# Gate and up of a feed-forward as seven block products of half the columns, and the projection down in three parts

## The reference

```
y = swiglu(rmsnorm(h, pre_g), w_gu, w_down)     # (silu(u @ gate) * (u @ up)) @ w_down
h = h + 0.5 * rmsnorm(y, post_g)                # first block; in the second h = h + y
```

## Time and profile before

| | |
|---|---|
| median of 3 runs | 3500.77 us (3498.62 to 3511.09) |
| profiled execution | 3503.76 us |
| its span, first to last instruction | 3501.9 us |
| TensorE busy | 3446.2 us, 98% |
| VectorE busy | 1805.0 us, 52% |
| ScalarE busy | 1373.8 us, 39% |
| GpSimd busy | 340.5 us, 10% |

### The profile page before, as it was taken

One profiled execution on the slowest core, in us unless ns is written; L12 is line 12 of the kernel. 1 busy time (PEld: TensorE's weight loads), 2 busy tenths in 40 slices (PEclk: granted clock), 3 DMA queues, 4 the chain that ended last, 5 costly groups with the idle time before them and its releaser, 6 DMA issues.

```text
span 3501.9 us, 42768 instructions
## 1 busy us (share of the span) xinstructions
PE 3446.2 (98%) x17080; PEld 2869.9 (82%) x17080; DVE 1805.0 (52%) x3164; ACT 1373.8 (39%) x2437; POOL 340.5 (10%) x327
## 2 busy tenths in 40 slices
PE   8999999999999999999999999999999999999998
PEld 7888887878888888888887878888888888888887
DVE  5442665746544335442665656544348675644432
ACT  4222453635432234222453544432236373333221
POOL 0110110121011001110111021011000001201100
PEclk9999999999999999999999999999999999999999
DMA  4223342252232332223433253232323322323232
GB/s 139 96 93 96 99 113 79 70 139 88 88 102 96 91 96 91 95 93 95 117 82 91 65 150 94 79 103 96 95 79 93 88 77 69 106 90 102 96 89 74
DMA packets 110871, 332.23 MB, mean 95 GB/s; under 512 B 18248, under 2 KB 19016, under 8 KB 110672
## 3 DMA queue, kind: packets, MB, share of 16 engines
q1 hardware_dynamic: 98352, 306.82, 28.1%
q0 software_dynamic: 12320, 22.66, 3.1%
HBM read 306.23 MB, written 4.21 MB: 89 GB/s over the span
## 4 chain that ended last, share of the span: by engine, by line
PE 94%; DVE 2%; DMA 2%; ACT 2%; issue 1%; POOL 0%; SPq 0%; DVEq 0%; ACTq 0%
PE PS L706 92%; PE PS L1031 1%; DMA raw<-in_win 1%; ACT wh L1150 1%; DVE wl L1639 0%; DMA raw<-in_gu 0%; DVE stk L1920 0%; DMA tmp<-tmp 0%; ACT tmp L1150 0%; DVE tmp L1969 0%; DVE tmp L2347 0%; PE PS L1024 0%; ACT PT L1150 0%; ACT L1150 0%; DVE tmp L1987 0%
## 5 line engine op out<-in xcount | busy, mean ns | idle before, releaser
L706 PE MATMUL PS<-uh,wh 128*128 128x512 f32 (+1 forms) x3096 | 1180.7, 381 | 16.1 <-DVE ul L1667 11.9
L1639 DVE TENSOR_TENSOR wl<-raw,wh 128x1024 fp32r<-128x1024 f32 (+2 forms) x595 | 725.6, 1221 | 877.9 <-ACT wh L1150 875.7
L706 PE MATMUL PS<-uh,wl 128*128 128x512 f32 (+1 forms) x3096 | 1176.9, 380 | 0.0
L706 PE MATMUL PS<-ul,wh 128*128 128x512 f32 (+1 forms) x3096 | 1171.1, 378 | 0.0
L1150 ACT ACTIVATE wh<-raw 128x1024 fp32r<-128x1024 f32 (+2 forms) x595 | 584.1, 984 | 537.8 <-PE PS L706 494.0
L706 PEld LDWEIGHTS PS<-uh,wh 128*128 128x128 f32 x3096 | 583.9, 189 | 136.1 <-DVE wl L1639 10.2
L706 PEld LDWEIGHTS PS<-ul,wh 128*128 128x128 f32 x3096 | 584.6, 189 | 113.7
L706 PEld LDWEIGHTS PS<-uh,wl 128*128 128x128 f32 x3096 | 583.1, 188 | 110.4 <-issue 1.4
L706 PE MATMUL PS<-gh,wh 128*128 128x512 f32 (+1 forms) x968 | 363.6, 376 | 0.0
L706 PE MATMUL PS<-gh,wl 128*128 128x512 f32 (+1 forms) x968 | 362.1, 374 | 0.0
L706 PE MATMUL PS<-gl,wh 128*128 128x512 f32 (+1 forms) x968 | 359.6, 372 | 0.0
(11 more groups left out here) (223 smaller groups left out, 3664.4 us busy)
## 6 DMA issues: line engine op xcount, KB each, us to landing
raw<-in_gu SPq DMA_DIRECT2D x220, 512.0 KB, 3.4
raw<-in_win SPq DMA_DIRECT2D x139, 512.0 KB, 3.5
raw<-in_dn SPq DMA_DIRECT2D x80, 512.0 KB, 3.5
raw<-in_wbr SPq DMA_DIRECT2D x72, 256.0 KB, 2.6
raw<-in_dn SPq DMA_DIRECT2D x40, 384.0 KB, 3.1
raw<-in_wout SPq DMA_DIRECT2D x24, 512.0 KB, 3.4
raw<-in_wv SPq DMA_DIRECT2D x20, 512.0 KB, 3.5
stk<-stk SPq DMA_DIRECT2D x72, 128.0 KB, 2.6
```

Of the source, the lines that this page charges most:

```text
L706: return e.matmul(out, lhs, rhs, start=start, stop=stop, skip_group_check=True)
L1639: tt(wl[:, p % 4, 0:n], raw[:, p % 3, 0:n], wh[:, p % 4, 0:n], SUB).then_inc(*S.lo.up(("lo", p)))
```

## The change

For f = 0 to 3 (`PLAIN`) gate and up stay as they were. For f = 4 to 21 one `pair` replaces the two jobs. The weight is seen as 2x2 blocks: two halves of the depth (4 tiles each) by gate and up; the activation as 2x2 blocks: two halves of the depth by two halves of the tokens (256 each). Strassen's algorithm in Winograd's form gives the four result blocks from seven products in place of eight, each product 4 tiles deep and 256 columns wide: 12 matmuls of 256 columns. That takes sums of blocks on both sides.

* Activation side, once for each feed-forward: `scaled` (DVE) applies gain and `rb` beforehand, sixteen instructions of 256 columns; four sums of 1024 columns, two on DVE (`sum_of`) and two on POOL; seven splits of 1024 columns, high part on ACT (`high`), low part on DVE (`low_operand`).
* Weight side, for each pair: POOL makes four sums of 512 columns from the two loaded pieces (`sums`), and ACT and DVE split four "cuts" (first, sums12, sums43 of 1024 columns, last of 512) in place of two pieces.
* Result side, for each pair: ACT copies four partial results of 256 columns out of PSUM, DVE adds four times from PSUM with a copy, multiplies gate and up, and makes the low part as before. PE waits for some of the copies in the middle of a pair.

POOL's multiplication by `rb` stays for f = 0 to 3 alone. The `raw` ring has four buffers in place of three.

The projection down runs in three parts of depth 6, 8 and 8 (after f = 6, after f = 14, after f = 21; `PARTS`, `DEPTHS`), each part 8 jobs. Parts are added up in SBUF: ACT copies the first, DVE adds the second and third (`add_part`). The square for the norm reads SBUF, and the gain of the norm after the stage is no longer applied by ACT but by DVE in the passage between stages (a SCALAR_TENSOR_TENSOR in place of the TENSOR_TENSOR at L1701; in the passages after mixers too). `dn` 5, 6 and 7 are cut in halves, in place of `dn` 7 alone. Buffers are laid out anew to make room.

```diff
+            def pair(v, f):
+                job = JOBS["pair", v, f]
+                c, (a, b, g, d) = job.first, pair_banks(f)
+                def product(i, at, part, b, start):
+                    E.wait_ge(S.lo, "lo", c + at)
+                    E.wait_ge(S.dn, "operand", v, i)
+                    for k in range(4):
+                        s = 512 * part + P * k
+                        w1, w2 = wh[:, (c + at) % 4, s:s + P], wl[:, (c + at) % 4, s:s + P]
+                        x1, x2 = bh[:, i, 256 * k:256 * k + 256], bl[:, i, 256 * k:256 * k + 256]
+                        last = three(bank(b, 0, 256), w1, w2, x1, x2, start and k == 0, k == 3)
+                    return last
+                take(a, S.dv, "c22", v, f)
+                product(0, 0, 0, a, True).then_inc(*S.mm.up(("product", v, f, 1)))
...
+                product(2, 0, 1, g, True).then_inc(*S.mm.up(("product", v, f, 2), ("cut", c)))
+                E.wait_ge(S.aa, "copy", v, f, 0)
+                product(3, 1, 1, a, False).then_inc(*S.mm.up(("product", v, f, 6), ("cut", c + 1)))
...
 # ScalarE
+                for f in range(PLAIN, FT):
+                    c = JOBS["pair", v, f].first
+                    ahead(c + 2)
+                    copy(f, 0, 1)
+                    if f > PLAIN and f - 1 not in PARTS:
+                        high_g(f - 1)
+                    copy(f, 1, 5)
+                    ahead(c + 4)
+                    copy(f, 2, 6)
+                    ahead(c + 5)
+                    silu(f, ("c12", v, f))
+                    copy(f, 3, 4)
 # VectorE
+                    if i == 0:
+                        scaled(0)
+                        scaled(1)
+                    elif i == 2:
+                        sum_of(1)
+                        scaled(4)
+                        scaled(5)
+                    elif i == 4:
+                        sum_of(3)
...
+                    elif i == 7:
+                        for n in (3, 4, 5, 6):
+                            low_operand(n)
...
+                for f in range(PLAIN, FT):
+                    c = JOBS["pair", v, f].first
+                    if f > PLAIN and f - 1 not in PARTS:
+                        gated(f - 1)
+                    ahead(c + 2)
+                    if f - 1 not in PARTS:
+                        low_g(f - 1)
+                    ahead(c + 3)
+                    first_gate(f)
+                    ahead(c + 4)
+                    second_gate(f)
+                    ahead(c + 5)
 # GpSimd
+                times_norm(0)
+                times_norm(1)
+                E.wait_ge(S.dn, "made", v, 4)
+                tt(bf[:, 6, :], bf[:, 4, :], b12[:, :], SUB).then_inc(*S.pl.up(("made", v, 6)))
+                times_norm(2)
+                E.wait_ge(S.dn, "made", v, 3)
+                tt(bf[:, 5, :], bf[:, 3, :], b21[:, :], SUB).then_inc(*S.pl.up(("made", v, 5)))
+                sums(PLAIN, 12)
+                times_norm(3)
+                sums(PLAIN, 43)
+                for f in range(PLAIN + 1, FT):
+                    sums(f, 12)
+                    sums(f, 43)
 # the passage between stages, VectorE
-                            tt(r, y_u[:, m, cols], spread_bank(c), MUL)
+                            stt(r, y_u[:, m, cols], pcol(*POST[v], m), spread_bank(c), MUL, MUL)
```

More of the change, by code:

```diff
@@ L220, in __init__ @@
         self.kind = tag[0]
-        self.last = first + len(pieces) - 1
+        self.last = first + cuts - 1
 class Fill:
@@ L263, with add, add_pair @@
 POST = [("f1post", 0), ("mpost", 0), ("f2post", 0), ("f1post", 1), ("mpost", 1), ("f2post", 1)]
+PLAIN = 4
+PARTS = (6, 14)
+DEPTHS = (6, 8, 8)
 def plan():
[L268 to L272, removed]
+    jobs, pieces, cuts = {}, [], []
+    def add(tag, name, idx, kt, banks, chunks, k0=0):
+        jobs[tag] = Job(len(jobs), tag, len(cuts), [(name, idx, k0, kt)], kt, banks, chunks, 1)
+        cuts.append(("piece", len(pieces)))
+        pieces.append((name, idx, k0, kt))
+        return jobs[tag]
+    def add_pair(v, f, name, idx0, idx1):
+        mine = [(name, idx0, 0, 8), (name, idx1, 0, 8)]
+        jobs["pair", v, f] = Job(len(jobs), ("pair", v, f), len(cuts), mine, 8, [], [], 4)
+        cuts.extend((kind, len(pieces)) for kind in ("first", "sums12", "sums43", "last"))
         pieces.extend(mine)
-        return jobs[tag]
     fills = {}
@@ L868, in ffn @@
             def ffn(v):
-                order = [JOBS[a, v, f] for f in range(FT) for a in ("gate", "up")]
+                order = [JOBS[a, v, f] for f in range(PLAIN) for a in ("gate", "up")]
                 begin(v, order[:3], order[3], order[4])
@@ L872, in ffn @@
                     run(job, v)
-                for m in range(KT if v == 7 else 7):
+                for f in range(PLAIN, FT):
+                    pair(v, f)
+                    if f in PARTS:
+                        for m in range(KT):
+                            run(JOBS["part", v, m, PARTS.index(f)], v, "g")
+                for m in range(KT if v == 7 else 5):
                     run(JOBS["dn", v, m], v, "g")
@@ L896, in group_out @@
                         if k == 7:
[L897 removed]
+                            i.then_inc(*S.mm.up(("job", job.tag, 0), ("cut", p)))
             def values(v, st):
@@ L916, in values @@
                         if j == 4:
-                            ends.append(("piece", p))
+                            ends.append(("cut", p))
                         if ends:
@@ L1682, in boundary @@
                 held, p0 = held_of(v), first_of(v + 1)
+                mixed = ffn_of(v) is None
                 ahead(p0)
-                for job in held[:-1]:
-                    gather("post", v, job.tag[2], 0)
+                for job in held:
+                    if not mixed:
+                        add_part(job, 0)
+                    if job is not held[0]:
+                        gather("post", v, job.tag[2] - 1, 0)
                 rstd_half(v, 0)
```

454 lines of the change are left out of this document (314 added, 140 removed).

## The result

The kernel after takes 3532.91 us, median of 4 runs (3529.69 to 3537.09); the kernel before, run again beside it, 3502.07 (3498.62 to 3511.09). The ratio is 1.0085, 95% interval 1.0062 to 1.0108: slower, by 0.9%. The profiled execution took 3530.34 us, its span is 3528.5, which is 26.6 more than before.

A forecast was written before the change was run, and what follows sets the result against it. PE (TensorE), busy 98% of the span, was taken as the bound. Terms -117 + 112 + 7 + 4 + 12 + 3 = +21 us gave 3525, 3522 for the median; own range 3505 to 3545, with rivals 3470 to 3580.

The forecast's parts named there:

- gain of the pairs: Gate and up: 84 matmuls of 256 columns take 9.83 us in place of 11.13, over 90 pairs, -117 us.
- packing of a steady pair: Steady pairs: DVE and POOL's port work, 9.6 us against PE's 9.83, packs imperfectly; 0.05 us for 85 pairs, +4 us.
- entry: Start of each feed-forward's pairs: PE waits for operands, sums and copies, 22.4 us each, +112 us (bounds +72 and +125).
- last depth tile: Third part of the projection down: its last tile waits for f = 21, 1.3 us x 5, +7 us (0 to 9).
- passages: Between stages: DVE's extra work costs 2.5 us in four passages, 1 in two after mixers, +12 us (5 to 25).
- stage 0: Stage 0's entry: small DVE instructions and two ACT table loads of 1.28 us come on top, +3 us.
- step 1: Entry: DVE's work before job 3's result is out of PSUM, 11.7 us plus 2.1 behind POOL, lasts until +16.9.
- Step 3: Entry: POOL's wide sums (2.6 us assumed) and weight sums delay the sums12 split; first pair at +33.4, 8.0 us lost.
- step 4: First pair: fourth product waits for ACT's copy, 6.8 us; sixth for DVE's `low_operand` 3 to 6 and last cut, 2.5.
- the second rival: Steady pairs: DVE and POOL's port is the bound, 10.4 us a pair, entry 25; 3578 us in all; chance 0.22.
- The faster one: Start of feed-forwards: DVE and POOL collide less, 14.4 us lost each; 3478 us in all; chance 0.27.
- Products that each pay for their waits: Pairs: each of seven products starts some 0.1 us late, 63 us; 3585 in all; chance 0.06.

The follow-up runs named there:

- e4: Against the kernel after: POOL's four weight sums made over 16 columns in place of 512 for f of 5 and more; 3522.87 us, ratio to before 1.0059.
- e7: Against the kernel after: mixers load only three pieces ahead, so the fourth `raw` buffer is of no use to them; 3541.13 us, ratio to before 1.011.
- e5: Against the kernel after: POOL makes one of its four weight sums twice in pairs of f = 5 and more; 3574.93 us, ratio to before 1.0205.
- e8: Against the kernel after: DVE's instruction in the passage between stages leaves out the norm's gain, applied nowhere; 3525.11 us, ratio to before 1.0062.

## Why the prediction was right, point by point

The time, 3532.9 against 3522, lies in the forecast's own range of 3505 to 3545, and the mechanism was the right one: the entry into the pairs ate what the pairs gained. By its terms, in us:

| term | predicted | measured | from |
|---|---|---|---|
| gain of the pairs | -117 | -107 | 90 x (11.13 - 9.94) |
| packing of a steady pair | +4 | +2 | pairs over 9.94 outside stage 0; +5 with it, none in e4 |
| entry | +112 | +111 | 22.2 + 3 x 22.0 + 23.0, timelines |
| last depth tile | +7 | +6.5 | 5 waits of 1.3 |
| passages | +12 | some +14 | what is left of stages 2, 3 and 5, 3.4 each, x 4 |
| stage 0 | +3 | some +5 | 2.8 in four long pairs, the rest in its passage |
| mixers | 0 | -7 | stage lengths, e7 |
| start before the first `rb` | 0 | +2 | 43.41 - 41.19; 41.0 to 42.8 in the other runs |
| sum | +21 | +26 | 26.6 between the spans |

**The gain** is the term that was mis-sized most. A pair takes 9.94 us, 0.1183 for a matmul; the forecast took 0.117 from ten matmuls, and ten were too few. That is 0.11 us in a pair and 10 us in all. At 84 x 90 = 7560 matmuls, a thousandth of a us is 7.6 us: such a distance wants a hundred matmuls, not ten. So "the smaller tile costs nothing by itself" was not quite right either. Half of 0.232 is 0.116, and 7/8 of 11.13 would be 9.74 us; the measured 9.94 is 2% more, 18 us over the 90 pairs. It is also why the pair came out above the 9.8 to 9.9 that the prediction named as its sign.

The forecast was 6 us low by the spans, and that it was no more is partly luck: the 10 us missing in the gain stand against the 7 us that the mixers gave back, which the forecast didn't have at all. The medians lie 11 us apart because the profiled execution after is 2.6 us below its median, and the one before 3.0 above the median that the forecast used.

**The entry** came out step by step, in stage 2: 4.5 us late before job 7 (laid out 5.1), 7.8 before the first pair (8.0), 6.9 before the fourth product (6.8), 2.7 before the sixth (2.5), and 0.4 behind it; 22.2 in all (22.4). The times were +19.6 (+19.9), +32.9 (+33.4), +44.1 (+44.4) and +49.6 (+49.7). Two slips of about 0.3 us are in the layout and don't matter: step 1 adds up to +16.6, not +16.9, and PE's undisturbed places are 0.3 later than it has them. These are the rows on which it turns, DVE's, ACT's and POOL's part of the timeline:

```profile
993.12 1.23 DVE L1789 TENSOR_TENSOR wl<-raw,wh 128x1024 fp32r<-128x1024 f32 x1 [1.64 <-ACT wh L1259]
...
999.43 2.83 DVE L1968 TENSOR_TENSOR bl<-bf,bh 128x1024 fp32r<-128x1024 f32 x1
...
1005.84 1.23 DVE L1789 TENSOR_TENSOR wl<-ws,wh 128x1024 fp32r<-128x1024 f32 x1 [3.58 <-ACT wh L1259]
1006.99 0.68 DVE L1916 TENSOR_TENSOR tmp<-PS,rb 128x512 f32<-128x512 f32 x1
...
1015.90 7.25 DVE L1968 TENSOR_TENSOR bl<-bf,bh 128x1024 fp32r<-128x1024 f32 x4
...
1023.67 0.68 DVE L1789 TENSOR_TENSOR wl<-raw,wh 128x512 fp32r<-128x512 f32 x1
```

```profile
1004.76 1.06 ACT L1259 ACTIVATE wh<-ws 128x1024 fp32r<-128x1024 f32 x1 [3.63 <-POOL ws L2641]
...
1013.06 1.06 ACT L1259 ACTIVATE wh<-ws 128x1024 fp32r<-128x1024 f32 x1 [3.78 <-POOL ws L2647]
```

```profile
989.82 3.27 POOL L2652 TENSOR_TENSOR bf<-bf,b 128x1024 f32<-128x1024 f32 x1 [3.13 <-DVE bf L1949]
...
997.79 3.39 POOL L2655 TENSOR_TENSOR bf<-bf,b 128x1024 f32<-128x1024 f32 x1
...
1001.14 2.24 POOL L2639 TENSOR_TENSOR ws<-raw 128x512 f32<-128x512 f32 x1
...
1003.46 1.26 POOL L2641 TENSOR_TENSOR ws<-ws,raw 128x512 f32<-128x512 f32 x1
```

Read backwards from PE's start at 1007.73: it needs the bank that L1916 empties at 1006.99; that stands in DVE's order behind the split of sums12 at 1005.84, which needs ACT's of 1004.76, which waited 3.63 us for POOL's L2641. POOL was late through two wide sums and two narrow ones, all but the last narrow one lengthened by DVE's splits, as DVE's are by POOL's (2.83 us where the undisturbed one takes 1.23). Step 3 has this chain. POOL's wide sums took 3.27 and 3.39 us, which is the 2.6 assumed with a lengthening on top. The sixth product starts at 1024.41, just after DVE has ended the four low parts of operands 3 to 6 and that of the last cut (1023.67 + 0.68 = 1024.35), which is the last link of step 4. The experiments bear the cause out: operands at a quarter take 11.6 of the 22.2 us away, two operands 3.5, and more cover 16.2.

**Steady pairs.** The forecast was that the port's work is 9.6 us, just under PE's, and that DVE would show near 100% with 1024 splits near 1.8 us. After shows 97% and 1650 and 1981 ns. The Trainium skill, SBUF — State Buffer, "Who interferes with whom", has the two engines exclude each other; e4 and e5 agree with that (1218, 1650 and 2130 ns for one instruction of DVE as POOL's work grows). Taken to the letter it made the pair 10.4 us, the second rival. Where the two engines and not PE set the pace, a pair takes 10.17 us: the forecast's 9.6 is too small and 10.4 too large. The forecast had the port's work under PE's time, and it is 0.23 us over; what keeps PE busy is the lead, for the first two to seven pairs of a part. The 0.05 us for each of 85 pairs, given for imperfect packing, came to 0.06 (5.1 us in all, 2.8 of them in stage 0): the right size for another reason.

**The rivals.** The faster one needed an entry under 17 us: it was 22.2. The port-bound pair was to decide from 9.95 us on. The mean of the 85 pairs is 10.00, so its mechanism is there, and it cost 5 us and not 47; e5 shows what comes when the port has a little more to do. Products that each pay for their waits would have given 0.7 us in each pair; the steady pair has no gap in PE's 50.00 of 50 us.

**Passages and stage 0.** Stage 2 is 5.7 us longer. The pairs save 18 x 1.19 = 21.4, the entry costs 22.2, the last tile 1.3, one long pair 0.2, which leaves 3.4 for the passage; 2.5 was predicted. Stages 3 and 5 leave the same 3.4. Stage 7, which no passage follows, is 2.8 longer with 0.7 left over by the same sum, so most of the rest does sit there. Of the 3.4 the gain is 0.9 (e8), and PE waits 1.20 us for the first operand of the next stage; how the cost divides between the adds and `gather`s was not taken apart. Stage 0 is 10.8 us longer than before, 5 us more than stage 2. Four long pairs hold 2.8 of them, and these are gone with thin weight sums (e4), so they are POOL's sums against DVE's instructions there, the small ones among them (rows at the end). Most of the rest lies in its passage, 82.02 us from the first matmul of the third part to the next `rb` against 80.19, and there it stays with thin sums (82.04). In e5 and e7 it is 80.5, so it comes and goes between runs, and its cause isn't shown. The forecast had put in 3 for stage 0. The table loads of ACT that it also named were not tried.

**The buffer priced at nothing.** The change part by part had the fourth `raw` buffer at 0, argued from feed-forwards, where loads are early. Mixers use the same ring, and there ACT did wait for loads (36.4 us before). Those rows were there to be read.

## What to carry to other kernels

A trick that saves a fixed share of matmul time for each unit brings its fixed preparation with it, and in an already full kernel the preparation costs what its cover lacks: lay it out in the four engines' orders in full, and then choose how many plain units cover it, since here two more of them cost 2.4 us and brought 16.2. Where two engines hold each other up, one busy share says little: at 97% DVE delayed nothing in one stretch, and 0.23 us in each pair further on. Add up the exclusive work, compare it with the bound, and look at the last units before a pause, not only at those in the middle: work done ahead hides a shortage until it is used up. Price a per-instruction distance from a hundred instructions when it will be multiplied by thousands, and when a shared buffer ring grows, look at each stage that uses it.

## What the runs showed of the hardware

**The clock falls after PE's long waits.** Windows of 5 us in the entry of stage 2, kernel after (the granted clock is the number behind POOL's count: 0.72, 0.50, 0.50):

```profile
995.00:1000.00 5.00, 5.00 (x18) 3.96 (x17) 4.14 (x5) 2.96 (x4) 4.31 (x2) 0.72 0.30 105
1005.00:1010.00 5.00, 2.27 (x10) 2.28 (x11) 3.56 (x4) 2.39 (x3) 1.59 (x1) 0.50 0.02 5
1020.00:1025.00 5.00, 4.94 (x23) 4.65 (x23) 5.00 (x6) 1.88 (x3) 0.93 (x1) 0.50 0.00 0
```

```profile
1008.10 0.42 PE L778 MATMUL PS<-bh,wl 128*128 128x256 f32 x1
1008.32 0.42 PE L778 MATMUL PS<-bl,wh 128*128 128x256 f32 x1
...
1023.93 0.41 PE L778 MATMUL PS<-bl,wh 128*128 128x256 f32 x1
1024.41 0.58 PE L778 MATMUL PS<-bh,wh 128*128 128x256 f32 x1
```

After waits of 4 to 6 us the clock is at its lower level, 1.2 in place of 2.4 GHz, and matmuls of 256 columns come some 0.21 us apart in place of 0.118. The forecast had left it at 1.00, which the earlier trace rows showed for a PE that never waits. It cost little here, since in the stretches before the next wait PE would only have waited longer. That holds for the fourth and fifth product too: at 0.21 us a matmul they end just when the sixth may start, so in stage 2 that wait of 2.7 us is hidden in slow matmuls and only a gap of some 0.3 us shows between the last two rows. What is left is 0.4 us from 1024.41 to the second pair. With shorter waits it doesn't vanish: six plain, whose waits in stage 2 are 0.96 us at 1001.71 and 2.14 at 1006.93, still shows 0.75 between 1005 and 1010.

**A tiny instruction can be caught too.** In stage 0, where DVE's small instructions lie among POOL's sums, four of this line, with 4 columns each, take over 1 us; three others of them take 0.17. Two of the four:

```profile
170.88 1.29 DVE L2114 TENSOR_SCALAR small<-small 128x4 f32<-128x4 f32 x1
172.40 1.15 DVE L2114 TENSOR_SCALAR small<-small 128x4 f32<-128x4 f32 x1
```

```profile
170.85 1.29 POOL L2639 TENSOR_TENSOR ws<-raw 128x512 f32<-128x512 f32 x1 [2.63 <-DVE wl L1789]
172.22 1.31 POOL L2641 TENSOR_TENSOR ws<-ws,raw 128x512 f32<-128x512 f32 x1
```

Each ends with the sum of POOL that was under way, so here an instruction with a single tensor input from SBUF is held up like one with two. The pair that holds them and the next one took 11.17 and 11.01 us in place of 9.94, 2.3 us of what stage 0 has on top.
